# Expert 31's first loads in quarters, expert 30's sums ahead of the last down product, the last MB as sixteen loads of eight partitions

## What is computed

```python
def moe(h, router_w, router_b, w_gate, b_gate, w_up, b_up, w_down, b_down):
    ...
    for e in range(N_EXPERTS):
        gate = jnp.minimum(hf @ w_gate[e] + b_gate[e], SWIGLU_LIMIT)
        up = jnp.clip(hf @ w_up[e] + b_up[e], -SWIGLU_LIMIT, SWIGLU_LIMIT)
        act = gate * jax.nn.sigmoid(SWIGLU_ALPHA * gate) * (up + 1.0)
        y = y + combine[:, e:e + 1] * (act @ w_down[e] + b_down[e])
```

## Time and profile before

| | us |
|---|---|
| median of three runs | 1166.03 |
| span of the profiled execution | 1165.3 |
| PE busy (share of the span) | 1122.3 (96%) |
| VectorE busy | 367.8 (32%) |
| ScalarE busy | 256.7 (22%) |
| DMA, mean rate over the span | 382 GB/s |
| HBM read | 443.47 MB |

### The profile page before, as it was taken

How to read it: one execution, slowest core, us unless ns; L and a number is a source line. 1 busy time by engine, 2 the same in 40 slices (tenths; PEclk the granted TensorE clock), 3 DMA queues, 4 the chain that set the end, 5 groups by cost and what they waited for, 6 DMA issues and landing times.

```text
span 1165.3 us, 15045 instructions
## 1 busy us (share of the span) xinstructions
PE 1122.3 (96%) x6121; PEld 559.3 (48%) x6121; DVE 367.8 (32%) x895; ACT 256.7 (22%) x528; POOL 15.6 (1%) x20
## 2 busy tenths in 40 slices
PE   9999999999999999898989899999999999999998
PEld 8998989864343434242424233333343433443333
DVE  5577765641223122122222212121212121222213
ACT  5566554431111111011111111111110111111002
POOL 1000000000000000000000000000000000000000
PEclk9999999999999999999999999999999998999999
DMA  9756566899999999999999999999999999999994
GB/s 300 224 174 189 163 205 245 308 408 422 424 428 420 431 432 431 431 431 431 431 431 431 431 429 431 430 429 431 430 431 431 431 430 432 427 428 429 423 423 203
DMA packets 53070, 445.52 MB, mean 382 GB/s; under 512 B 3747, under 2 KB 32089, under 8 KB 35985
## 3 DMA queue, kind: packets, MB, share of 16 engines
q1 hardware_dynamic: 50954, 439.83, 91.0%
q0 software_dynamic: 1248, 4.20, 1.4%
q10 hardware_dynamic: 806, 0.59, 0.2%
HBM read 443.47 MB, written 1.13 MB: 382 GB/s over the span
## 4 chain that ended last, share of the span: by engine, by line
PE 70%; DMA 26%; DVE 2%; issue 1%; ACT 1%; ACTq 0%; SPq 0%; DVEq 0%
PE psum L1365 26%; DMA ring<-in_w_up 25%; PE psum L1394 14%; PE psum L1288 5%; PE psum L988 4%; PE psum L989 4%; PE psum L990 4%; PE psum L1303 4%; PE psum L1311 2%; PE psum L1035 1%; PE psum L1128 1%; PE psum L1104 1%; ACT pieces L741 1%; PE psum L1296 1%; PE psum L1082 1%
## 5 line engine op out<-in xcount | busy, mean ns | idle before, releaser
L1365 PE MATMUL psum<-ring,xT 128*64 128x512 f32 x960 | 436.4, 611 | 35.9 <-DMA ring<-in_w_up 35.3
L1366 PE MATMUL psum<-ring,xT 128*64 128x512 f32 x960 | 436.5, 611 | 0.0
L1365 PEld LDWEIGHTS psum<-ring,xT 128*64 128x64 f32 x960 | 132.5, 141 | 316.0 <-issue 279.3
L1394 PE MATMUL psum<-ring,guT 128*64 128x512 f32 x984 | 226.2, 602 | 0.4 <-DVE guT L1864 0.4
L1845 DVE COPY gu<-psum 128x512 f32<-128x512 f32 x32 | 33.5, 1047 | 574.5 <-PE psum L1366 574.5
L1366 PEld LDWEIGHTS psum<-ring,xT 128*64 128x64 f32 x960 | 132.5, 141 | 0.0
L1394 PEld LDWEIGHTS psum<-ring,guT 128*64 128x64 f32 x984 | 65.6, 137 | 135.4 <-issue 113.3
L928 ACT COPY gu<-psum 128x512 f32<-128x512 f32 x32 | 34.0, 1061 | 419.7 <-PE psum L1366 419.7
L1533 DVE TENSOR_TENSOR pieces<-raw,pieces 128x2048 fp32r<-128x2048 f32 x31 | 71.1, 2297 | 34.5 <-ACT pieces L741 34.5
L988 PE MATMUL psum<-hT_hi,pieces 128*128 128x256 f32 x272 | 78.3, 288 | 0.1
L989 PE MATMUL psum<-hT_lo,pieces 128*128 128x256 f32 x272 | 76.9, 283 | 0.0
(11 more groups left out here) (208 smaller groups left out, 1026.0 us busy)
## 6 DMA issues: line engine op xcount, KB each, us to landing
ring<-in_w_down SPq DMA_DIRECT2D x25, 4096.0 KB, 20.9
ring<-in_w_up SPq DMA_DIRECT2D x24, 4096.0 KB, 29.0
ring<-in_w_gate SPq DMA_DIRECT2D x23, 4096.0 KB, 30.2
ring<-in_w_up SPq DMA_DIRECT2D x14, 2048.0 KB, 14.8
ring<-in_w_gate SPq DMA_DIRECT2D x12, 2048.0 KB, 19.9
raw<-in_w_in SPq DMA_DIRECT2D x22, 1024.0 KB, 5.5
ring<-in_w_down SPq DMA_DIRECT2D x7, 2048.0 KB, 13.3
ring<-in_w_down SPq DMA_DIRECT2D x12, 1024.0 KB, 19.9
```

The lines of the kernel that those rows point to most:

```text
L1365: mm(every(bank(GU + nb)[0:CAP, :]), x_k, of_chunks(gate[:, k, :], nb), start=k == 0, stop=k == KC - 1)
L1366: done = mm(every(bank(GU + nb)[CAP:P, :]), x_k, of_chunks(up[:, k, :], nb), start=k == 0, stop=k == KC - 1)
L1394: done = mm(o[half * CAP:(half + 1) * CAP, :], values[:, k, :], chunk_k[:, half * BANK:(half + 1) * BANK], start=k == 0, stop=k == KC - 1)
```

## The change

Three edits, in the last two experts only.

1. The first half of gate 31 and up 31 comes as two quarters: gate 0 to 1 and up 0 to 1 (on `tail_in[2]`), gate 2 to 3 and up 2 to 3 (on a new `tail_in[11]`), in place of four chunks of gate and then four of up. PE waits for `tail_in[11]` ahead of chunk 2.
2. `y_taken`, the sums of expert 30 and the turn of expert 31's spread stand ahead of the whole down product of expert 31, not between its halves.
3. The last MB (chunks 6 and 7 of down 31) is sixteen loads of eight partitions, all on `last_in[1]`, whose threshold rises from 16 to 256 on the first pass.

```diff
+LAST = [HALF, HALF + HALF // 2, KC]
+FEW = 8
...
-        tail_in = [sem(f"tail_in{i}") for i in range(11)]
-        last_in = [sem(f"last_in{i}") for i in range(2)]
+        tail_in = [sem(f"tail_in{i}") for i in range(12)]
+        last_in = [sem(f"last_in{i}") for i in range(len(LAST) - 1)]
...
+                        if k == 1:
+
+                            for m in both:
+                                load(m, 0, HALF // 2, tail_in[2])
+                            for m in both:
+                                load(m, HALF // 2, HALF, tail_in[11])
+                            continue
...
-                for half in range(2):
-                    load(TAIL + 5, HALF + half * HALF // 2, HALF + (half + 1) * HALF // 2, last_in[half])
+                load(TAIL + 5, LAST[0], LAST[1], last_in[0])
+                for p0 in range(0, P, FEW):
+                    r = slice(p0, p0 + FEW)
+                    sp.dma_start(ring[(TAIL + 5) % RING][r, LAST[1]:, :].rearrange("p c n -> p (c n)"),
+                                 weights_of[2][E - 1][r, LAST[1]:, :].rearrange("p c n -> p (c n)")).then_inc(last_in[1], 16)
...
+                        if m0 == TAIL + 2 and k == HALF // 2 and nb == 0:
+                            pe.wait_ge(tail_in[11], 32 * (p + 1))
...
+                y_taken(it + 1)
+                for tt in range(TT):
+                    add_to_tokens(tt)
+                turn_spread(it + 1)
                 for h in range(PARTS):
...
-                    y_taken(it + 1)
-                    for tt in range(TT):
-                        add_to_tokens(tt)
-                    turn_spread(it + 1)
-
-                    def halves(k):
-                        c = k - h * HALF
-                        if c % (HALF // 2) == 0:
-                            pe.wait_ge(last_in[c // (HALF // 2)], 16 * (p + 1))
-
-                    down_part(bank(GU), h, ring[(TAIL + 5) % RING], hidden, halves)
+
+                    def as_it_lands(k):
+                        if k in LAST:
+                            loads = P // FEW if k == LAST[1] else 1
+                            pe.wait_ge(last_in[LAST.index(k)], p * (16 * loads) + 16 * loads)
+
+                    down_part(bank(GU), h, ring[(TAIL + 5) % RING], hidden, as_it_lands)
```

## The result

The changed kernel takes 1170.18 us (median of six runs, 1169.22 to 1173.5) against 1166.16 for the one before (six runs, 1164.6 to 1167.09). The profiled execution has a span of 1168.1 us where before had 1165.3.

What follows compares the result with a forecast made beforehand. The weight stream sets the pace through the expert loop, and PE bounds the tail. Quarters -1.3, exposed copy +0.86, one change of kind fewer -0.1 sum to -0.5 us: 1165.5 from 1166.03, range 1163.9 to 1168.0.

Steps and rivals of the forecast that it cites:

- Where the time stands before: In the last two experts: PE stalls for a load, 4.2 us with the slow clock; at most 2.3 us can be won.
- (a) quarters: Expert 31's gate and up: earlier first quarters remove 4.2 us, three new waits return 2.9; 1.3 us faster.
- the stall: At expert 31's first product: PE waits 2.49 us for the first half of the up matrix.
- the low clock: Behind the wait at expert 31's first product: granted clock 0.60 from 1121.9 to 1126.2, costing 1.7 us.
- (b) sums ahead: Before down 31: PE waits for the copy of expert 30's output, +0.86 us; one change of kind fewer, -0.1.
- (c) sixteen loads of eight partitions: Last MB of down 31: issues done in time, eight engines a load, no cost if those are the early engines.
- The last MB is late: Rival at down 31's last two chunks: late engines carry the small loads, +0.7 us, 1166.2; chance 0.27.
- The issues starve the end: Rival on SyncE's queue: each small load costs 2.1 us to issue, the last chunks start at 1163, 1175; chance 0.05.
- The clock falls anyway: Rival in the tail: the new waits lower PE's clock behind 1136.7, costing 1.7 us, 1167.2; chance 0.12.
- The first quarter isn't earlier: Rival at expert 31's first product: the wait there stays and the copy is exposed, 1166.03 + 0.76 = 1166.8; chance 0.06.

Runs made afterwards that it cites:

- rows16: The changed kernel with its last MB as eight loads of sixteen neighbouring partitions instead of sixteen loads of eight; 1169.51 us, ratio 1.0035.
- only_quarters: The kernel before with the first edit alone, expert 31's first half in quarters; 1165.38 against 1166.08 us, ratio 0.9996.
- only_sums: The kernel before with the second edit alone, expert 30's sums ahead of the last down product; 1166.43 against 1166.08 us, ratio 1.0004.
- one_last: The changed kernel with its last MB as one load of 128 partitions again; 1166.38 against 1165.37 us, ratio 1.0006.
- places_fourth: The changed kernel with small loads written to every fourth partition of a block of 32, the rows read still eight neighbours; 1168.58 us, ratio 1.0028.
- every_fourth: The changed kernel with each of the sixteen small loads taking every fourth partition of a block of 32; 1168.57 against 1166.02 us, ratio 1.0025.
- high_first: every_fourth with the eight loads to partitions 64 to 127 ahead of those to 0 to 63; 1171.15 us, ratio 1.0037.
- only_sixteen: The kernel before with the third edit alone, its last MB as sixteen loads of eight partitions; 1171.44 us, ratio 1.0055.

## Why the prediction was wrong, step by step

- *Where the time stands before* and *(a) quarters* held against the profile of before. The last quarter came at 12.49 us after the end of 29's sums (forecast 12.5), down 30 at 17.5 (17.4). PE didn't start at once but waited 0.41 us for VectorE's guT, which I had overlooked behind the stall of before. It was luck that this cost nothing: the waits for the later loads took it up, the one ahead of the third quarter (forecast 0.7, none stated in the changed kernel, 0.51 in rows16) first. Waits of 1.31 and 0.76 us stood where 1.5 and 0.8 were forecast. The term was -1.3; only_quarters' profile shows -1.2. But in these profiles all of that is the low clock, which I took as bound to follow the stall: only_sums' profile has the stall without it and reaches down 30 0.2 us sooner than only_quarters does.
- *(b) sums ahead* held: +0.76 us (0.86 - 0.1) was forecast, and 19.20 against 18.44 us from down 30 to the last sums is what only_sums and one_last show, with a stated wait of 0.69 or 0.68 us on ScalarE's copy of y_half. The sum of (a) and (b), -0.5, is -0.44 in one_last's profile. The times of one_last (1.0006, or -0.3 to +1.9 us) don't show it. The low clock is a likely reason, and not a shown one: where it doesn't follow the stall, (a) wins nothing and (b) still costs 0.76, and how often it does no run counts.
- *(c) sixteen loads of eight partitions* is the step that failed. The issues were over in time (0.72 us each, 1.3 was the point from which they would decide), and the completions were eight a load. Whether the early engines carried the small loads, as the forecast needed, wasn't measured. But I gave each of eight engines 16 rows in place of 8 at the old price of a row, 0.31 us, and so bounded the delay of the last MB by 2.5 us and its effect by 0.7. That price was the error. The last MB came 5.1 us later (1156.36 against 1151.3), because from between 1140 and 1142 on the rows in flight took 1.6 times as long (median 0.50 us), and the ordinary third quarter landed 4 us late too. The unasked question was where in SBUF the eight rows of a load go. In place of "nothing", or at most 0.7 us, the term is 3.1 us by the stretches (39.75 - 36.66); the times, 1.0042 against 1.0006, put it at some 4 us. That alone takes the time past the range's end at 1168.0.
- *The rivals.* "The last MB is late" had the right place and symptom, a wait before the last two chunks, but the wrong mechanism and under a quarter of its price (0.7 of 3.1 us); no rival priced a row that gets slower. "The issues starve the end" foresaw the sign and is refuted by the 11.57 us. "The clock falls anyway" isn't seen in the changed kernel, though the low clock is there in four experiments, behind waits of 2.26 to 3.37 us in the last product, which none of the forecast waits reached. "The first quarter isn't earlier" is refuted by the row at 1119.79.

The sentence that would have warned stood in the Trainium skill, "SBUF — State Buffer", section "Can I just issue two DMAs to hit both halves?": "The only way to hit all 16 ports is one transfer spanning all 128 partitions." I had priced only how many engines a small load uses. The runs agree with it for neighbours and differ in one point: loads of 64 partitions, every second, and of 32, every fourth, do as well as one of 128 (1.0001 and 0.9998).

## What to carry to other kernels

Split a load along its free dimension, or, if it must be by partitions, so that each piece touches every group of four neighbours (every second or every fourth of all 128 partitions). Pieces that left groups out cut the rate of all that was in flight from 417 GB/s to between 210 and 256 in most stretches here. When DMA rows look alike in size, compare GB/s divided by the DMA share before and after; if it falls, the engines are held up and not out of work. At the end of a stream such a hold-up is paid in full, since nothing behind it can take it up: 1 MB loaded in such pieces cost over 3 us of 1166. And before a stall is priced together with the low clock behind it, more than one execution has to show that clock: here it was worth the whole 1.2 us that the quarters won.

## What the runs showed of the hardware that was not expected

- A load to few partitions slows the others too: the ordinary third quarter landed 4 us late, and the full-share rate of all engines together fell from 417 to between 213 and 256 GB/s in nine kernels whose small loads leave groups of four partitions out (271 and 277 in places_fourth and every_fourth), though these loads were 1 MB at the stream's end.
- Which half of the partitions such a load goes to matters, for a reason that wasn't measured: in every_fourth and high_first the full-share rate was 338 to 350 GB/s while the eight loads to partitions 0 to 63 had their turn and 210 to 220 with the eight to 64 to 127, in either order.
- A wait of 2.5 us on PE was followed by a granted clock of 0.60 over the next 4.3 us in two kernels (before, only_sixteen) and of 1.00 in a third (only_sums), though PE's instructions up to there are the same.
